# The first feed-forward's last output tile in two halves of the tokens

## The reference, cut to what matters

```python
# end of the first block
x = x + rms_norm(conv_glu_ffn(h, ffn_up, ffn_conv, ffn_down), g[5])
#   conv_glu_ffn ends in (gelu(g) * val) @ w_down      (512 x 2816) @ (2816 x 1024)
#   rms_norm(y, g) = y * rsqrt(mean(y * y over the 1024 channels) + 1e-6) * g

# start of the second block
hn = rms_norm_2(h, attn_norm)        # h is the x of above, with 16 meta tokens before it
proj = hn @ w_in                     # its first pieces: c_q (256 wide), c_kv (128), k_rope (32)
```

## Time and profile before

| | us |
|---|---|
| median of 3 runs | 1901.83 |
| lowest and highest | 1897.15, 1903.69 |
| the profiled execution: device time | 1900.31 |
| the profiled execution: span in the trace | 1898.5 |
| PE busy (share of the span) | 1815.4 (96%) |
| DVE busy | 1018.2 (54%) |
| ACT busy | 732.4 (39%) |
| POOL busy | 295.0 (16%) |

### The profile page before, as it was taken

One profiled execution on the slowest core, in us unless ns is written; L12 is line 12 of the kernel. 1 busy time (PEld: TensorE's weight loads), 2 busy tenths in 40 slices (PEclk: granted clock), 3 DMA queues, 4 the chain that ended last, 5 costly groups with the idle time before them and its releaser, 6 DMA issues.

```text
span 1898.5 us, 22254 instructions
## 1 busy us (share of the span) xinstructions
PE 1815.4 (96%) x8983; PEld 1456.3 (77%) x8983; DVE 1018.2 (54%) x1518; ACT 732.4 (39%) x1220; POOL 295.0 (16%) x235
## 2 busy tenths in 40 slices
PE   8999999999999998989999999899878999999998
PEld 5778876788888876778888888787656788888887
DVE  6777845444454366357777722574365534444322
ACT  4433343332334444344444422445356533222221
POOL 2013501011212040141111100500100101111100
PEclk9999999999999999999999999999978899999999
DMA  5222322232224421122222222231300122222221
GB/s 190 89 78 89 101 89 78 78 112 98 91 93 153 143 94 40 67 78 88 90 90 100 83 106 100 91 110 69 106 12 32 56 91 98 89 100 89 100 89 56
DMA packets 49829, 171.13 MB, mean 90 GB/s; under 512 B 5882, under 2 KB 8570, under 8 KB 49600
## 3 DMA queue, kind: packets, MB, share of 16 engines
q1 hardware_dynamic: 45216, 155.69, 23.8%
q0 software_dynamic: 3936, 13.51, 2.1%
q10 hardware_dynamic: 576, 0.52, 0.1%
HBM read 165.51 MB, written 4.19 MB: 89 GB/s over the span
## 4 chain that ended last, share of the span: by engine, by line
PE 82%; DVE 6%; ACT 5%; issue 4%; POOL 2%; DMA 0%; SPq 0%; DVEq 0%; POOLq 0%; ACTq 0%
PE ps L377 26%; PE ps L379 25%; PE ps L378 25%; PE ps L382 3%; PE ps L2600 2%; ACT ws_h L305 1%; POOL sums L424 1%; DVE ws_l L313 1%; PE ps L2617 1%; ACT P L2724 1%; POOL x L1441 1%; DMA x<-in_x 0%; PE ps L2612 0%; DVE tmp L815 0%; ACT x L1144 0%
## 5 line engine op out<-in xcount | busy, mean ns | idle before, releaser
L313 DVE TENSOR_TENSOR ws_l<-raw,ws_h 128x1024 fp32r<-128x1024 f32 x289 | 394.4, 1369 | 522.4 <-ACT ws_h L305 521.9
L377 PE MATMUL ps<-h_h,ws_h 128*128 128x512 f32 (+1 forms) x1448 | 582.3, 402 | 19.4 <-DVE h_l L548 10.3
L379 PE MATMUL ps<-h_h,ws_l 128*128 128x512 f32 (+1 forms) x1448 | 571.2, 394 | 0.0
L378 PE MATMUL ps<-h_l,ws_h 128*128 128x512 f32 (+1 forms) x1448 | 570.9, 394 | 0.0
L305 ACT ACTIVATE ws_h<-raw 128x1024 fp32r<-128x1024 f32 x289 | 303.4, 1054 | 448.9 <-PE ps L379 446.0
L377 PEld LDWEIGHTS ps<-h_h,ws_h 128*128 128x128 f32 x1448 | 276.4, 191 | 93.4 <-issue 16.1
L379 PEld LDWEIGHTS ps<-h_h,ws_l 128*128 128x128 f32 x1448 | 276.6, 191 | 61.6
L378 PEld LDWEIGHTS ps<-h_l,ws_h 128*128 128x128 f32 x1448 | 278.4, 192 | 58.5
L377 PE MATMUL ps<-G_h,ws_h 128*128 128x512 f32 (+1 forms) x374 | 142.9, 382 | 1.1 <-DVE ws_l L313 1.1
L379 PE MATMUL ps<-G_h,ws_l 128*128 128x512 f32 (+1 forms) x374 | 142.6, 381 | 0.0
L378 PE MATMUL ps<-G_l,ws_h 128*128 128x512 f32 (+1 forms) x374 | 142.6, 381 | 0.0
(11 more groups left out here) (437 smaller groups left out, 2418.9 us busy)
## 6 DMA issues: line engine op xcount, KB each, us to landing
raw<-in_ffn_up SPq DMA_DIRECT2D x88, 512.0 KB, 3.2
raw<-in_w_merge SPq DMA_DIRECT2D x36, 512.0 KB, 3.2
raw<-in_ffn_down SPq DMA_DIRECT2D x22, 512.0 KB, 3.2
raw<-in_w_down SPq DMA_DIRECT2D x22, 512.0 KB, 3.2
raw<-in_w_hy SPq DMA_DIRECT2D x12, 512.0 KB, 4.0
raw<-in_w_sc SPq DMA_DIRECT2D x12, 512.0 KB, 3.3
raw<-in_fwd SPq DMA_DIRECT2D x8, 512.0 KB, 3.3
raw<-in_w_naqk SPq DMA_DIRECT2D x8, 512.0 KB, 3.2
```

Source lines behind the costliest of these rows:

```text
L313: dve.e.tensor_tensor(w.lo, raw[n % NRAW][:], w.hi, ALU.subtract).then_inc(*lo_made.says(("lo", n)))
L377: pe.e.matmul(o, a.hi, b.hi, start=start, stop=False, skip_group_check=True)
L378: pe.e.matmul(o, a.hi, b.lo, start=False, stop=False, skip_group_check=True)
L379: return pe.e.matmul(o, a.lo, b.hi, start=False, stop=stop, skip_group_check=True)
```

## The change

The last tile of `"r5"` is made in two halves of 256 tokens. PE first fetches all 22 weight blocks of the tile (the list `ws`, which waits for all three chunks), makes the 22 products for tokens 0 to 255 (part 0), then the 22 for tokens 256 to 511 (part 1), with the same weights. Among part 1's products stand part 0's sum (after k = 3) and its spread (after k = 10). Part 1's own sum and spread follow its last product. ACT, DVE and POOL do the steps for 256 tokens of each tile, part 0 first and then part 1. h is made as before, a whole tile at a time, when both halves of x are there. The two chunks that were split during tile 7 are now split behind part 0's steps, on ACT as on DVE, since the weights of tile 7 stay in use.

```diff
-        for m, k in DOWN:
+        for m, k in DOWN[:-22]:
...
+        ws = [(blocks.next(), blocks.c) for k in range(22)]
+        for part in range(2):
+            v = ("r5", part)
+            o = bank((v, 7), Ring(place, [bank_at["r5", part]]))
+            for k, (w, c) in enumerate(ws):
+                i = mm(o[:, 0:256], w, G1[:, k, halves[part]], k == 0, k == 21)
+                if part == 1 and k == 3:
+                    total_of_tokens(("r5", 0), bank(("sum", ("r5", 0)), rings["seven"]), 2, 0)
+                if part == 1 and k == 10:
+                    spread_tokens(("r5", 0), bank(("spread", ("r5", 0)), rings["seven"]))
+                if part == 1 and k < 21 and ws[k + 1][1] != c:
+                    i.then_inc(*products.says(over(c)))
+            i.then_inc(*products.says(("done", (v, 7)), over(c) if part else None))
+        total_of_tokens(("r5", 1), bank(("sum", ("r5", 1)), rings["seven"]), 2, 1)
+        spread_tokens(("r5", 1), bank(("spread", ("r5", 1)), rings["seven"]))
...
+    def residual_halves_act(v, prev, nv, gain, dst, early):
+        load_roots()
...
+        for part in range(2):
+            u, at = (v, part), halves[part]
+            act.wait_ge(("done", (u, 7)))
+            act.e.activation(eighth[:, at], out_of((u, 7))[:, 0:256], ACT.Square).then_inc(*squared.says(("sq", u, 7)))
+            root_of_tokens(u, D)
+            if part:
+                early()
+                act.wait_ge(("rs", u, 0))
+            act.wait_ge(("done", ("spread", u)))
+            act.e.activation(rstd[:, at], out_of(("spread", u))[:, 0:256], ACT.Copy).then_inc(
+                *act_out.says(("scale", u), ("free", ("spread", u))))
+            if not part:
+                split_hi(used["act"] + 1)
+                split_hi(used["act"] + 2)
...
+        for m in range(8):
...
+            act.wait_ge(("x half", v, m))
+            h_part(nv, m, gain, dst(m), ("x", v, m), H_FREE[nv])
+            square(nv, m, x[:, m, :], L, (v, 1), True, slots)
...
+    def residual_halves_dve(v, gain, nv, ngain, dst, early):
+        inverse_of_tokens((v, 0))
+        for part in range(2):
+            u, at = (v, part), halves[part]
+            if part:
+                split_lo(used["dve"] + 1)
+                split_lo(used["dve"] + 2)
+                inverse_of_tokens(u)
+                early()
+            for m in range(8):
+                i, old = rings["dve T"].take(("rs", u, m))
+                src, free = half_tile(v, part, m)
...
+                dve.e.scalar_tensor_tensor(T[i][:, 0:256], src, P(gain, m), factor, ALU.mult, ALU.mult).then_inc(
+                    *dve_out.says(("rs", u, m), free))
+                if part and m == 0:
+                    dve.wait_ge(("rs", u, 0))
+                    dve.e.tensor_tensor(x[:, 0, at], x[:, 0, at], T[i][:, 0:256], ALU.add).then_inc(
+                        *dve_part.says(("x", v, 0), ("gone", ("rs", u, 0))))
+                if part and m == 1:
+                    h_rest(nv, 0, ngain, dst(0))
+                elif part and m > 2:
+                    h_rest(nv, m - 2, ngain, dst(m - 2))
...
+    def residual_halves_pool(v, nv):
+        for part in range(2):
+            u, at = (v, part), halves[part]
+            for m in range(part, 8):
+                pool.wait_ge(("rs", u, m))
+                pool.e.tensor_tensor(x[:, m, at], x[:, m, at], t_slot(("rs", u, m))[:, 0:256], ALU.add).then_inc(
+                    *pool_part.says(("x" if part else "x half", v, m), ("gone", ("rs", u, m))))
+        squares_pool(nv)
```

32 lines of the change are left out of this document (26 added, 6 removed).

## The result

| | before | after |
|---|---|---|
| median, us | 1902.69 | 1907.02 |
| lowest and highest of 20 runs each | 1897.15, 1909.36 | 1903.43, 1912.92 |
| the profiled execution: device time | 1900.31 | 1905.68 |
| the profiled execution: span | 1898.5 | 1903.6 |

The ratio of the times is 1.0032, with a 95% interval from 1.0021 to 1.0043. So the change costs 4 to 8 us; the medians alone lie 4.3 us apart. The time lies within the range given, but the forecast was a loss of 2.7 us that would pass as no change, and the interval leaves no change out: the loss is 1.5 to 3 times the forecast.

What follows compares the result with a forecast made beforehand. PE, busy for 96% of the span, was taken as the bound. Products' end +2.7, chain behind it +0.3 and stream -0.3 gave +2.7 us: span 1901.2, expected median 1904.5 us, range 1899.5 to 1908.5.

Steps and rivals of the forecast that it cites:

- Parts 1 to 5: From tile 7's first product to the next block's: cost of halves, late start, sum and spread, chain, DVE; restart 3.0 us later.
- The stall: At tile 7's start PE waits for DVE's split of chunk 21, as all 22 blocks are fetched first: 1.28 us lost.
- the price of the halves: Tile 7's products: 132 matmuls at 0.117 take 15.4 us, as 66 at 0.233; only some 0.2 us for restarts.
- the two splits beside POOL: Behind part 0's steps, DVE's two weight splits run beside POOL's last three additions and take 3.25 us.
- DVE's queue: Eight steps of part 0, then two splits, stand ahead of part 1's reciprocal, which starts 2.8 us behind its data.
- part 4: Chain behind the last product were DVE free: PE restarts near 1206.4, 0.7 us later than 1205.66, the best possible.
- Part 6: Next block's first product to k = 3: 5.6 us in place of 5.88, as h arrives faster; gain 0.3 us.
- Nothing outside of the seam changes but the numbers of the PSUM banks.: Outside the stretch around tile 7 and the next block's start, only bank numbers differ; no time counted for it.
- DVE and POOL hindering each other: Rival: part 0's additions take 1.05 us each, splits and h come later, clock stays low; 7.4 us loss, 1909.2; chance 0.13.
- splits free of POOL: Rival: additions take 0.63 us and the two splits 2.3; k = 3 is 1.3 us late, 1903.1; chance 0.20.
- clock stays up: Rival: DVE's queue empty in time and PE's clock high after the cut idle stretch; 0.8 us faster, 1901.0; chance 0.05.
- something behind 1211 that waits today no longer does: Sign against the forecast: a present wait vanishing after about 1211 us, where PE was taken as dense; no size given.

Runs made afterwards that it cites:

- e1_lazy: Changed kernel with each weight block of the last tile fetched at first use in part 0; tile 6's last matmul to next norm's sum 49.54 us, against 50.61.
- e4_halves: Kernel before with only the last tile's products in two halves, all 22 blocks fetched first; tile 6's last matmul to next norm's sum 49.71 us, against 47.32.
- e3_early: Changed kernel with one of the two weight splits moved ahead of part 0's steps; tile 6's last matmul to next norm's sum 49.28 us, against 50.61.
- e2_recip: Changed kernel with part 1's reciprocal ahead of the two weight splits on DVE; restart 27.41 us after tile 6's last matmul, against 27.26.
- w_after: Changed kernel with matmuls of ones, results unread, in PE's idle time: 8 ahead of part 1's spread, 9 behind it; ratio to kernel before 1.0027.
- w_before: Kernel before with 15 matmuls of ones, results unread, behind the spread in PE's idle time; ratio to kernel before 1.0007.
- b_wait: Kernel before with the attention's first scores made to wait for the fifth copy of V; ratio to kernel before 1.0017.
- s_after: Changed kernel with the PSUM banks of tile 7's halves exchanged, so the scores wait for the fourth copy of V again; ratio to kernel before 1.0034.
- d_delay: Kernel before with one idle DVE reciprocal of 3.35 us, result unread, ahead of the first residual step; ratio to kernel before 1.0024.
- s_best: Changed kernel with blocks fetched at first use, weight splits and early() moved on DVE, and tile 7's banks exchanged; ratio to kernel before 1.0015.

## Why the prediction was wrong, and where it was right

**Parts 1 to 5 held.** Counted from tile 6's last matmul (1181.51 in the forecast, 1178.92 in the profile):

| | forecast | after |
|---|---|---|
| first product | 1.51 | 1.51 |
| last product | 18.22 | 18.22 |
| part 0's eighth step ends | 19.5 | 19.9 |
| reciprocal starts | 22.8 | 22.7 |
| spread starts | 23.1 | 23.0 |
| restart | 27.2 | 27.26 |
| k = 3 | 32.8 | 33.44 |
| sum for the next norm | 50.0 | 50.6 |

The stall (e1_lazy), the price of the halves (e4_halves), the two splits beside POOL (3.25 forecast, 2.99 measured) and DVE's queue (e3_early) are confirmed. The trace agrees with the rule of the Trainium skill, "SBUF — State Buffer", section "Who interferes with whom", by which a VectorE instruction with two inputs in SBUF and a GpSimd instruction that reads SBUF are in each other's way: the two splits took 2.99 us, not 2.3. One reading was off: I wrote as if the late reciprocal were the link that holds PE up. e2_recip moved it 2.8 us ahead and nothing came of it, since the splits stand ahead of part 1's steps anyway. And one sum of part 4 doesn't come out: 2.1 us later and 0.7 won is 1.4 later than 1205.66, so 1207.1 and not "near 1206.4". It served only for the best case, not for the forecast.

**Part 6 failed in size.** I counted a gain of 0.3 us between restart and k = 3, from h that comes faster. It took 6.18, 5.74 and 6.53 us in the three profiles of after, against 5.88, 5.89 and 5.89 before. Nothing was gained and 0.3 lost on average. I had counted six matmuls at half clock; of the first 18 behind the restart, 10, 8 and 12 were issued at 0.50 in after's three profiles (7, 7 and 9 in before's). w_after, without the low clock, took 4.56, so faster h was worth more than I thought, and the clock took it back. I had also put before's waits for h at 0.5 us; w_before, at clock 1.00 and still 5.89 us long, shows that h set the pace there and not the clock. With this the seam is 3.15 us longer, not 2.7.

**The step that failed is "Nothing outside of the seam changes but the numbers of the PSUM banks."** The numbers are an order, and the order decides which copy a later bank waits for: 0.4 us at the attention's first scores. This much is shown: the wait is 1.05 to 1.11 us in every profile with the new order or with b_wait's edit, and 0.67 or 0.68 in all others, s_after among them. Of the ten profiles with this longer wait, eight have a fall of the clock in the same place, for 3.4 us or more with the wait. Taken over three profiles each, the time behind the seam is 3.17 us longer than the reference profile's in after and 1.32 in before, so 1.85 us of the loss lie there. With 3.15 that is 5.0 us, near the 5.3 to 6.1 us of the ratios. But "behind" varies from 0.38 to 4.71 between profiles of the same kernel after, so that share rests on six profiles and is a size, not a cause.

**The chances.** The sum gave 2.7 us, and I weighed "slower by more than 0.3%" at 0.13, through one rival (DVE and POOL hindering each other), which didn't happen: part 0's steps, which wait for the additions, stood 0.68 to 0.70 us apart. Only its clause on the clock came half true: behind after's restart the clock stayed low for 4.2, 3.2 and 4.9 us, in before's three profiles for 3.0, 2.9 and 3.6. What I left out is that a delay of PE may be paid at the clock as well. d_delay would fit that: 3.5 us of seam gave 1.0024, which is 4.6 us. By its interval, 2.3 to 6.7 us, 3.5 would do as well, so that surcharge isn't shown. The rivals "splits free of POOL" and "clock stays up" are refuted by 2.99 us and by the clock of 0.50. Of what would show me wrong I named "something behind 1211 that waits today no longer does"; it was the reverse, a wait that grew.

**What stays open:** whether the longer bank wait, or the clock's later return at the seam, causes the fall of the clock at 1284 to 1292, or only goes with it. So of the 5 to 6 us, 3.15 at the seam and the 0.4 of the wait are explained, the rest is not. No version beats the kernel before. The nearest with the tile in halves is s_best, with a seam 0.8 us shorter than the mean of before's three and a ratio of 1.0015 [0.9998, 1.0033].

## What to carry to other kernels

Splitting a last tile so that the norm of its first half runs beside the second pays only if the engines of the norm have room there: here the products had to start later (1.28 us), carried sum and spread (1.17 us), and DVE's queue was longer at the moment it mattered. When an engine's late step looks like the culprit, ask what stands between it and the next consumer on the same engine: moving the step alone (e2_recip) bought nothing. A change in the order of a ring of banks is an edit of every later wait on that ring, so list those waits before calling it free.
